# Two rotated projections: one product for the sine, the weights' high part on ScalarE, five places and a direct bank read in the local mixer

## The chip, the cores and the metric

The program runs on one core of a Trainium2 chip. The metric is the device time of one launch in microseconds (us); lower is better. PE is TensorE (matmuls), DVE is VectorE, ACT is ScalarE, POOL is GpSimd, SP is SyncE, which issues the loads here.

## What is computed

Two layers of a block with four parallel mixers. Only two of them matter here: differential attention ("a", 16 groups of width 32 for q and k together) and the windowed attention, the local mixer ("d", 6 groups of width 64). Both norm and rotate their q and k:

```python
def rmsnorm(x, g):
    y = xf * lax.rsqrt(jnp.mean(xf * xf, axis=-1, keepdims=True) + EPS)
    return (y * g).astype(x.dtype)

def _rotate(xh, ang):
    x1, x2 = jnp.split(xh, 2, axis=-1)
    return jnp.concatenate([x1 * cos - x2 * sin, x1 * sin + x2 * cos], axis=-1)

def axial_rope(x, rows, cols):      # first half of the width turned by the row, second by the column
    return concatenate([_rotate(x[..., :hd // 2], ang_r), _rotate(x[..., hd // 2:], ang_c)])

for l in range(DEPTH):              # DEPTH = 2
    px, pcx = split_cols(hx @ w_in[l]), split_cols(hc @ w_in[l])     # 1024 latent and 256 context tokens, D_MODEL 1024
    a_l, a_c = diff_attention(...); b_l, b_c = mlstm_mixer(...); c_l, c_c = gla_mixer(...); d_l, d_c = window_gqa(...)
    y = concatenate([a_l, b_l, c_l, d_l]) * silu(px[15]);  x = x + gt * (y @ w_out[l])
```

## The kernel before

The stages of a layer run one after the other, with a barrier of all engines between them. Each stage is written out by hand, engine by engine; the order in the code is the order on the engine, and counting semaphores tie the engines together. Nothing is planned by a scheduler.

`project_qk` is the stage in question. It runs four times: for "a" and for "d", in each of the two layers. The 1280 tokens are ten tiles of 128, in two halves of five (HN = 5). The product of the normed input (`hT`, channels by tokens) and a weight slab (`ring`) is made in split precision by `SplitProduct`: each operand is parted into a high part (rounded to F32R) and the low rest, and PE makes three matmuls where one would do. It goes by steps: a step is one group g (a half of the tokens and a slab) and one k of the eight 128-channel chunks. "a" has four groups (two halves with the 512 q and k columns, two halves with the 256 v columns), so 32 steps; "d" has two groups of 512 columns (384 of q and k, 128 of v), so 16 steps. I number the steps from 0. A step of 512 columns is 15 matmuls of 512 columns, a step of 256 columns is 15 of 256. For every step

- ACT makes the input's high part (`high`, line L418),
- DVE makes the weights' high part (L381), the weights' low part (L382) and then the input's low part (L435, `low`),
- PE waits for all of them and multiplies (`multiply`, L454).

The parts have three places, so that the parts of step i can be made when PE has done step i - 3.

Between the steps, work on the previous half is woven in (`half_step`): ACT squares the sums in the banks (L1427) and copies v (L1431) and q and k (L1432, to `raw`, which has five places); DVE adds the squares (L1495); ACT takes the root in two activations (L1443 and L1444, each with a table load); DVE refines it (L196 to L199, `refine`) and norms the tile (L1509). Then POOL multiplies by the gain (L1480) and makes the cosine product into `rot` (L1485), DVE makes the sine product into `turn` as four products of a quarter each (L1520) and adds both (L1528 in "a", L1534 in "d").

`rot` has two places. In "a" a place is free when DVE has added. In "d" the sum is left in `rot`, PE transposes it (`turns`, L1401, banks 6 and 7), ACT copies the result to `qkT` (L1418), and a place of `rot` is free only when PE has turned it (`turned`). PE turns tiles 0 and 1 between steps 14 and 15, and all others after step 15. In "d" the second half of the tokens has no later steps to lie beside; it is worked off after step 15.

Of the kernel before, what the change touches and what calls it, by code (L numbers as in the profile page):

```python
# [23 lines left out]
P = 128  # L24
# [360 lines left out]
class SplitProduct:  # L385
# [4 lines left out]

    def __init__(self, nc, env, own, name, groups, bufs=2):
        self.env, self.groups, self.BUFS = env, groups, bufs
        self.steps = [(g, k) for g in range(len(groups)) for k in range(KT)]
        self.first = [sum(len(q[5]) for q in groups[:g]) for g in range(len(groups) + 1)]
        self.hi, self.lo, self.weights, self.dv, self.used, self.ready, self.read = (
            env["signal"](f"{name}_{n}") for n in ("x_hi", "x_lo", "w_parts", "split", "parts_used", "sum_ready", "sum_read"))
        toks, cols = max(q[4] for q in groups), max(q[2] for q in groups)
# [12 lines left out]
    def high(self, act, i):  # L412

        g, k = self.steps[i]
        _, _, _, t0, m, _ = self.groups[g]
        if i >= self.BUFS:
            self.wait_used(act, i - self.BUFS)
        act.activation(self.x_hi[:, i % self.BUFS, 0:m], self.env["hT"][:, k, t0:t0 + m], ACT.Copy).then_inc(self.hi.sem, 1)  # L418

    def low(self, dve, i):  # L420

        g, k = self.steps[i]
        s, c0, w, t0, m, _ = self.groups[g]
        at = i % self.BUFS
        if k == 0 and (g == 0 or self.groups[g - 1][0] != s):
            dve.wait_ge(self.env["loaded"][s].sem, 16)
        if i >= self.BUFS:
            self.wait_used(dve, i - self.BUFS)
        split_weights(dve, slab(self.env, s)[:, k, c0:c0 + w], self.w_hi[:, at, 0:w], self.w_lo[:, at, 0:w], self.dv)\
            .then_inc(self.weights.sem, 1)  # L430
        if k == KT - 1 and (g + 1 == len(self.groups) or self.groups[g + 1][0] != s):
            dve.wait_ge(self.weights.sem, i + 1)
            dve.sem_inc(self.env["slab_used"].sem, 1)
        dve.wait_ge(self.hi.sem, i + 1)
        dve.tensor_tensor(self.x_lo[:, at, 0:m], self.env["hT"][:, k, t0:t0 + m], self.x_hi[:, at, 0:m].bitcast(F32),  # L435
                          ALU.subtract).then_inc(self.lo.sem, 1)
# [905 lines left out]
def project_qk(nc, env, name, s_qk, groups, width, qkT, v_of, last_slab_next, halves=None):  # L1342
# [4 lines left out]
    ps, signal = env["ps"], env["signal"]  # L1347
    n_qk = groups * width
    nch = n_qk // P
    sq_ready, reduced, ms_ready, root, normed, gained, cos_ready, rotated, dv, turned, kept = (  # L1350
        signal(f"{name}_{n}") for n in ("square", "reduced", "mean", "root", "normed", "gained", "cos", "rotated",
                                        "dve", "turned", "turned_kept"))
    s_v, v0, nv, v_dst = v_of
    HN = NT // 2
    HT = HN * P
# [4 lines left out]
    with ExitStack() as own, nc.Block() as block:  # L1360
# [8 lines left out]
        if halves:  # L1369
            rot = tile("rot", [P, 2, n_qk])  # L1370
        else:
            rot = spare[:, 3 * n_qk:5 * n_qk].rearrange("p (u c) -> p u c", u=2)
        stat = tile("stat", [P, 3, HN * groups])
        ms, rstd, tmp = (stat[:, i, :] for i in range(3))
        proj = SplitProduct(nc, env, own, f"{name}_proj", plan, 3)
        cos = C(env, f"cos_{name}").rearrange("p (t w) -> p t w", t=NT)
        sin = C(env, f"sin_{name}").rearrange("p (t w) -> p t w", t=NT)
        q4 = width // 4
# [16 lines left out]
        def _(pe):  # L1395
            def turns(t):
                pe.wait_ge(rotated.sem, t + 1)
                if t >= 2:
                    pe.wait_ge(kept.sem, t - 1)
                for c in range(nch):  # L1400
                    last = pe.transpose(ps[:, 6 + t % 2, c * P:(c + 1) * P], rot[:, t % 2, c * P:(c + 1) * P], C(env, "ident"))  # L1401
                last.then_inc(turned.sem, 1)

            for i, (g, k) in enumerate(proj.steps):
# [9 lines left out]
        def _(act):  # L1414
# [6 lines left out]
            def keep(t):  # L1421
# [40 lines left out]
            if s_v == s_qk:  # L1462
                for a in range(HN):
                    keep(HN + a)
                roots(1)
            else:
# [6 lines left out]
            act.wait_ge(proj.read.sem, proj.first[-1])  # L1473

        @block.gpsimd
        def _(pool):
            for t in range(NT):
# [12 lines left out]
        def _(dve):  # L1490
# [13 lines left out]
                rsqrt_newton(dve, dv, rstd, ms, tmp)  # L1504

            def norm(t):
                dve.wait_ge(proj.read.sem, t + 1)
                x = grouped(raw[:, t % HN, :])
                dve.tensor_tensor(x, x, of_tile(rstd, t).unsqueeze(2).broadcast_to([P, groups, width]), ALU.mult)\  # L1509
                   .then_inc(normed.sem, 1)  # L1510

            def rotate(t):
# [11 lines left out]
                dve.wait_ge(cos_ready.sem, t + 1)  # L1524
                if halves:
                    for i, half in enumerate(halves):
                        a, b = (x.rearrange("p (s i c) -> p s i c", s=2, i=2)[:, :, i, :] for x in (rot[:, t % 2, :], turn[:, :]))
                        ins = dve.tensor_tensor(half[:, t, :].rearrange("p (s c) -> p s c", s=2), a, b, ALU.add)  # L1528
                        if i == 0:
                            dv.mark(ins)  # L1530
                    dve.wait_ge(dv.sem, dv.n)
                    ins.then_inc(rotated.sem, 1)
                else:
                    dve.tensor_tensor(rot[:, t % 2, :], rot[:, t % 2, :], turn[:, :], ALU.add).then_inc(rotated.sem, 1)  # L1534

            def half_step(h, k):

# [912 lines left out]
```

## Time and profile before

| | us |
|---|---|
| median of 3 runs | 2687.75 (2673.01 to 2691.18) |
| the profiled execution, whole | 2683.7 |
| its span | 2681.9 |
| "a" in layer 0 | from 537 to 661 in the span |
| "d" in layer 0 | from 929 to 1029 in the span |

PE is busy for 2151.8 us, DVE for 1867.3, ACT for 1129.8 and POOL for 411.4 us of the span. The profile has parts on engines, on 40 slices of time, on DMA, a chain of waits, and groups of instructions by line. The trace behind it gives, for a stretch of time, who waited for whom, and every instruction with its start, its duration and, in brackets, the idle time of its engine before it and what ended that.

### The profile page before, as it was taken

The numbers are of one execution on the slowest core, as the hardware profiler recorded it, in microseconds if no ns is written. First come the engines' busy times: TensorE is split into PE (matmuls) and PEld (weight loads), VectorE is DVE, ScalarE is ACT, GpSimd is POOL, SyncE is SP. The second block draws the span as 40 slices with busy tenths as digits, with TensorE's granted clock in tenths as the row PEclk, the third lists the DMA queues.
The fourth block names the chain that finished last, engine by engine and source line by source line (L and its number), as shares of the span: only waits on it lengthen the run. The fifth ranks groups of instructions, "written<-read, shape, count | busy, mean of one in ns | idle before, by whom it ended". The sixth has DMA issues, their size and how long they took to land. (4 is left out here: it accounts for less than half of the span.)

```text
span 2681.9 us, 38569 instructions
## 1 busy us (share of the span) xinstructions
PE 2151.8 (80%) x14712; PEld 1804.3 (67%) x14712; DVE 1867.3 (70%) x3533; ACT 1129.8 (42%) x2196; POOL 411.4 (15%) x410
## 2 busy tenths in 40 slices
PE   4968798786888785899978778879767977858988
PEld 2857676666677664787857567767655866647877
DVE  2585667778878567755745766669698786667757
ACT  4433351333667534633224443432435666346321
POOL 0002204322000011022110004025031000110222
PEclk7978896898898797999988889969788989979999
DMA  8100010000000100001433000100000001000021
GB/s 322 74 16 1 17 48 2 2 1 1 1 1 1 48 32 1 29 36 39 153 138 120 16 16 2 48 16 2 1 0 1 1 1 48 16 17 27 37 104 54
DMA packets 18182, 99.80 MB, mean 37 GB/s; under 512 B 2128, under 2 KB 2256, under 8 KB 12752
## 3 DMA queue, kind: packets, MB, share of 16 engines
q1 hardware_dynamic: 12816, 87.89, 8.6%
q10 hardware_dynamic: 5184, 9.44, 0.9%
q8 instruction: 119, 1.95, 0.3%
q14 instruction: 63, 0.52, 0.1%
HBM read 87.88 MB, written 9.44 MB: 36 GB/s over the span
## 5 line engine op out<-in xcount | busy, mean ns | idle before, releaser
L1807 DVE TENSOR_REDUCE a_st<-ps 128x1 f32<-128x1280 f32 (+1 forms) x144 | 196.9, 1370 | 23.2 <-PE ps L1719 22.7
L1778 ACT ACTIVATE ring<-ps,a_st 128x1280 f32<-128x1280 f32 (+1 forms) x144 | 177.3, 1232 | 74.6 <-DVE a_st L1807 74.4
L454 PE MATMUL ps<-a_proj_wh,a_proj_xh 128*128 128x512 f32 (+1 forms) x320 | 119.2, 373 | 62.5 <-DVE a_proj_xl L435 61.6
L2090 PE MATMUL ps<-g_x_hi,g_w_hi 128*128 128x512 f32 (+1 forms) x400 | 148.4, 371 | 10.0 <-DVE g_x_lo L2151 9.5
L2091 PE MATMUL ps<-g_x_lo,g_w_hi 128*128 128x512 f32 (+1 forms) x400 | 147.7, 369 | 0.0
L2092 PE MATMUL ps<-g_x_hi,g_w_lo 128*128 128x512 f32 (+1 forms) x400 | 147.6, 369 | 0.0
L1719 PE MATMUL ps<-a_k,a_q 128*128 128x512 f32 (+1 forms) x400 | 123.8, 419 | 26.1 <-ACT ring L1778 21.6
L2151 DVE TENSOR_TENSOR g_x_lo<-hT,g_x_hi 128x512 fp32r<-128x512 f32 (+1 forms) x120 | 84.5, 709 | 85.3 <-ACT g_x_hi L2114 83.8
L2114 ACT ACTIVATE g_x_hi<-hT 128x512 fp32r<-128x512 f32 (+1 forms) x120 | 70.3, 589 | 158.3 <-PE ps L2092 151.2
L1734 PE MATMUL ps<-cst,ring 128*128 128x128 f32 x656 | 107.8, 299 | 27.0 <-ACT a_aT L1787 15.1
L418 ACT ACTIVATE b_proj_xh<-hT 128x640 fp32r<-128x640 f32 (+1 forms) x64 | 63.8, 1003 | 147.4 <-PE ps L454 145.0
L2225 PE MATMUL ps<-o_w_hi,o_y_hi 128*128 128x512 f32 x288 | 114.1, 396 | 13.5 <-DVE o_y_lo L2256 7.2
L2164 POOL TENSOR_TENSOR yT<-yT,g_gate 128x512 f32<-128x512 f32 (+1 forms) x50 | 61.3, 1232 | 382.5 <-DVE g_gate L2129 236.7
L454 PEld LDWEIGHTS ps<-a_proj_wh,a_proj_xh 128*128 128x128 f32 x320 | 68.7, 215 | 75.3 <-issue 48.9
L454 PE MATMUL ps<-a_proj_wl,a_proj_xh 128*128 128x512 f32 (+1 forms) x320 | 116.2, 363 | 0.0
L454 PE MATMUL ps<-a_proj_wh,a_proj_xl 128*128 128x512 f32 (+1 forms) x320 | 115.8, 362 | 0.0
L2226 PE MATMUL ps<-o_w_lo,o_y_hi 128*128 128x512 f32 x288 | 113.5, 394 | 0.0
L2227 PE MATMUL ps<-o_w_hi,o_y_lo 128*128 128x512 f32 x288 | 113.3, 393 | 0.0
L1734 PEld LDWEIGHTS ps<-cst,ring 128*128 128x128 f32 x656 | 81.4, 153 | 46.5 <-ACT a_aT L1787 22.9
L454 PE MATMUL ps<-b_proj_xh,b_proj_wh 128*128 128x512 f32 (+1 forms) x192 | 76.9, 401 | 44.4 <-DVE b_proj_xl L435 38.0
L418 ACT ACTIVATE a_proj_xh<-hT 128x640 fp32r<-128x640 f32 x64 | 46.6, 741 | 147.9 <-PE ps L454 145.6
L2282 ACT ACTIVATE o_y_hi<-yT 128x640 fp32r<-128x640 f32 (+1 forms) x64 | 43.5, 686 | 152.5 <-PE ps L2227 144.6
(363 smaller groups left out, 6397.9 us busy)
## 6 DMA issues: line engine op xcount, KB each, us to landing
ring<-in_w SPq DMA_DIRECT2D x22, 2048.0 KB, 7.5
yT<-in_w SPq DMA_DIRECT2D x4, 2048.0 KB, 9.8
latents<-hT ACTq DMA_DIRECT2D x32, 256.0 KB, 2.0
ring<-in_w SPq DMA_DIRECT2D x6, 1024.0 KB, 5.0
hT<-in_tok SPq DMA_DIRECT2D x10, 512.0 KB, 15.5
hT<-in_tok SPq DMA_DIRECT2D x20, 256.0 KB, 5.9
hT<-latents SPq DMA_DIRECT2D x16, 256.0 KB, 6.5
cst<-in_cst SPq DMA_DIRECT2D x1, 2688.0 KB, 14.6
```

The lines of the kernel that those rows point to most:

```text
L418: act.activation(self.x_hi[:, i % self.BUFS, 0:m], self.env["hT"][:, k, t0:t0 + m], ACT.Copy).then_inc(self.hi.sem, 1)
L454: last = pe.matmul(out, left, right, start=k == 0 and j == 0, stop=k == KT - 1 and j == 2)
L1719: last = pe.matmul(ps[:, 3 * c + b, 0:w], q4[:, 2 * h + c, t * P:(t + 1) * P], k4[:, 2 * h + c, k0:k0 + w], start=True, stop=True)
L1734: last = pe.transpose(ps[:, 6 + n % 2, (k - a) * P:(k - a + 1) * P], p(u, 0, T)[:, k * P:(k + 1) * P], C(env, "ident"))
L1778: act.activation(p(u, c, n), ps[:, 3 * c:3 * c + 3, :].rearrange("p b n -> p (b n)")[:, 0:n], ACT.Exp, bias=st[:, 0:1], accum_out=st[:, 1: ...
L1807: dve.tensor_reduce(stat[:, u % SLOTS, c, 0:1], ps[:, 3 * c:3 * c + 3, :].rearrange("p b n -> p (b n)")[:, 0:n], AX.X, ALU.max, negate=Tru ...
L2090: pe.matmul(out, w_hi[:, k, cols], x_hi[:, at, 0:b[1]], start=k == 0, stop=False)
L2091: pe.matmul(out, w_hi[:, k, cols], x_lo[:, at, 0:b[1]], start=False, stop=False)
L2092: last = pe.matmul(out, w_lo[:, k, cols], x_hi[:, at, 0:b[1]], start=False, stop=k == KT - 1)
L2225: pe.matmul(ps[:, n % 8, :], y_hi[:, at, tile], w_hi[:, at, :], start=k == 0, stop=False)
L2226: pe.matmul(ps[:, n % 8, :], y_hi[:, at, tile], w_lo[:, at, :], start=False, stop=False)
L2227: last = pe.matmul(ps[:, n % 8, :], y_lo[:, at, tile], w_hi[:, at, :], start=False, stop=k == KT - 1)
```

## The change

Five edits, all in `SplitProduct` and `project_qk`; both "a" and "d" have the first two, "d" alone the others:

1. The sine product is one instruction over the whole tile, with the axis of the two quarters read backwards, instead of four.
2. The weights' high part is made by ACT, ahead of the input's high part of the same step (`act_weights`); DVE waits for it before it makes the low part.
3. `rot` in "d" has five places instead of two. They lie in `yT[:, 6:8]` instead of the spare end of `ring`. POOL's cosine product of the first five tiles waits for no turn.
4. The second half of "d" (`late`): ACT doesn't copy q and k to `raw`; DVE's norm reads them from the banks and writes `raw`.
5. The second half of "d": DVE makes the cosine product, POOL only the gain.

```diff
     def high(self, act, i):
...
+        if self.act_weights:
+            s, c0, w = self.groups[g][0:3]
+            if k == 0 and (g == 0 or self.groups[g - 1][0] != s):
+                act.wait_ge(self.env["loaded"][s].sem, 16)
+            act.activation(self.w_hi[:, i % self.BUFS, 0:w], slab(self.env, s)[:, k, c0:c0 + w], ACT.Copy).then_inc(self.w_high.sem, 1)
         act.activation(self.x_hi[:, i % self.BUFS, 0:m], self.env["hT"][:, k, t0:t0 + m], ACT.Copy).then_inc(self.hi.sem, 1)
...
     def low(self, dve, i):
...
-        split_weights(dve, slab(self.env, s)[:, k, c0:c0 + w], self.w_hi[:, at, 0:w], self.w_lo[:, at, 0:w], self.dv)\
-            .then_inc(self.weights.sem, 1)
+        if self.act_weights:
+            dve.wait_ge(self.w_high.sem, i + 1)
+            dve.tensor_tensor(self.w_lo[:, at, 0:w], slab(self.env, s)[:, k, c0:c0 + w], self.w_hi[:, at, 0:w].bitcast(F32),
+                              ALU.subtract).then_inc(self.weights.sem, 1)
...
-            rot = spare[:, 3 * n_qk:5 * n_qk].rearrange("p (u c) -> p u c", u=2)
+            rot = env["yT"][:, 6:8, :].rearrange("p a t -> p (a t)")[:, 0:HN * n_qk].rearrange("p (u c) -> p u c", u=HN)
+        SLOTS = 2 if halves else HN
...
-        proj = SplitProduct(nc, env, own, f"{name}_proj", plan, 3)
+        proj = SplitProduct(nc, env, own, f"{name}_proj", plan, 3, act_weights=True)
...
+        def late(t):
+
+            return not halves and t >= HN
...
                 act.activation(sq[:, t % 2, :], bank[:, 0:n_qk], ACT.Square).then_inc(sq_ready.sem, 1)
+                if late(t):
+                    act.activation(v_dst(t), bank[:, v0:v0 + nv], ACT.Copy).then_inc(v_kept.sem, 1)
+                    return
...
-                if t >= 2:
-
-                    pool.wait_ge(rotated.sem if halves else turned.sem, t - 1)
-                pool.tensor_tensor(grouped(rot[:, t % 2, :]), grouped(x),
+                if late(t):
+                    continue
+                if t >= SLOTS:
+
+                    pool.wait_ge(rotated.sem if halves else turned.sem, t - SLOTS + 1)
+                pool.tensor_tensor(grouped(rot[:, t % SLOTS, :]), grouped(x),
...
-                dve.tensor_tensor(x, x, of_tile(rstd, t).unsqueeze(2).broadcast_to([P, groups, width]), ALU.mult)\
+                if late(t):
+                    dve.wait_ge(v_kept.sem, t - HN + 1)
+                    dve.wait_ge(rotated.sem, t - HN + 1)
+                dve.tensor_tensor(x, grouped(ps[:, t % BANKS, 0:n_qk]) if late(t) else x, of_tile(rstd, t).unsqueeze(2).broadcast_to([P, groups, width]), ALU.mult)\
...
-                for i in range(2):
-                    for f in range(2):
-                        ins = dve.tensor_tensor(y[:, :, f, i, :], x[:, :, f, 1 - i, :],
-                                                s[:, f, i, :].unsqueeze(1).broadcast_to([P, groups, q4]), ALU.mult)
-                        dv.mark(ins)
+                dv.mark(dve.tensor_tensor(y, x[:, :, :, ::-1, :], s.unsqueeze(1).broadcast_to([P, groups, 2, 2, q4]), ALU.mult))
+                if late(t):
+                    if t >= SLOTS:
+                        dve.wait_ge(turned.sem, t - SLOTS + 1)
+                    dv.mark(dve.tensor_tensor(grouped(rot[:, t % SLOTS, :]), grouped(raw[:, t % HN, :]),
+                                              cos[:, t, :].unsqueeze(1).broadcast_to([P, groups, width]), ALU.mult))
+                else:
+                    dve.wait_ge(cos_ready.sem, t + 1)
                 dve.wait_ge(dv.sem, dv.n)
```

What stands in a row on DVE in "d", first half, from the norms of tiles 2 to 4 to the rotation of tile 0, before (`d_proj_wh`, `wl` and `xl` are the parts of step 13, `cst` holds the sines):

```order
L1509 TENSOR_TENSOR d_raw<-d_raw,d_stat 128x384 x3
L381 CAST d_proj_wh<-ring 128x512
L382 TENSOR_TENSOR d_proj_wl<-ring,d_proj_wh 128x512
L435 TENSOR_TENSOR d_proj_xl<-hT,d_proj_xh 128x640
L1520 TENSOR_TENSOR ring<-d_raw,cst 128x6x16 x4
L1534 TENSOR_TENSOR ring<-ring 128x384
```

And in the changed kernel:

```order
L1535 TENSOR_TENSOR d_raw<-d_raw,d_stat 128x384 x3
L437 TENSOR_TENSOR d_proj_wl<-ring,d_proj_wh 128x512
L446 TENSOR_TENSOR d_proj_xl<-hT,d_proj_xh 128x640
L1544 TENSOR_TENSOR ring<-d_raw,cst 128x384
L1562 TENSOR_TENSOR yT<-yT,ring 128x384
```

The cast has left DVE, four products are one, and the sum lands in `yT`.

DVE in "d", second half, from the last line of `refine` to the first rotation, before:

```order
L198 TENSOR_SCALAR d_stat<-d_stat 128x30
L199 TENSOR_TENSOR d_stat<-d_stat 128x30
L1509 TENSOR_TENSOR d_raw<-d_raw,d_stat 128x384 x5
L1520 TENSOR_TENSOR ring<-d_raw,cst 128x6x16 x4
L1534 TENSOR_TENSOR ring<-ring 128x384
```

And in the changed kernel:

```order
L198 TENSOR_SCALAR d_stat<-d_stat 128x30
L199 TENSOR_TENSOR d_stat<-d_stat 128x30
L1535 TENSOR_TENSOR d_raw<-ps,d_stat 128x384 x5
L1544 TENSOR_TENSOR ring<-d_raw,cst 128x384
L1548 TENSOR_TENSOR yT<-d_raw,cst 128x384
L1562 TENSOR_TENSOR yT<-yT,ring 128x384
```

The norms read the banks (`ps`), and the cosine product has come to DVE between the sine product and the sum.

## Rows read from the trace of the kernel before

**Rows 1.** The page: the span, and busy time with share and instructions.
```profile
span 2681.9 us, 38569 instructions
...
PE 2151.8 (80%) x14712; PEld 1804.3 (67%) x14712; DVE 1867.3 (70%) x3533; ACT 1129.8 (42%) x2196; POOL 411.4 (15%) x410
```

**Rows 2.** Who waited for whom, 535 to 662: us in total, times, longest.
```profile
PE ps L454 <- DVE a_proj_xl L435: 30.6, 11, 6.4
```

**Rows 3.** Instructions of DVE in order of time, "a", layer 0: start, duration.
```profile
562.22 0.43 DVE L381 CAST a_proj_wh<-ring 128x512 fp32r<-128x512 f32 x1 [1.51 <-PE ps L454]
...
578.71 1.52 DVE L381 CAST a_proj_wh<-ring 128x512 fp32r<-128x512 f32 x1
580.27 1.48 DVE L382 TENSOR_TENSOR a_proj_wl<-ring,a_proj_wh 128x512 fp32r<-128x512 f32 x1
581.67 1.90 DVE L435 TENSOR_TENSOR a_proj_xl<-hT,a_proj_xh 128x640 fp32r<-128x640 f32 x1
...
589.11 0.89 DVE L1520 TENSOR_TENSOR ring<-a_raw,cst 128x128 f32<-128x128 f32 x4
...
590.93 2.88 DVE L1520 TENSOR_TENSOR ring<-a_raw,cst 128x128 f32<-128x128 f32 x4
...
627.73 0.28 DVE L381 CAST a_proj_wh<-ring 128x256 fp32r<-128x256 f32 x1
```

**Rows 4.** Instructions of POOL, the same stage.
```profile
578.27 1.69 POOL L1480 TENSOR_TENSOR a_raw<-a_raw,par 128x512 f32<-128x512 f32 x1 [67.79 <-DVE a_raw L1509]
580.03 1.17 POOL L1485 TENSOR_TENSOR a_rot<-a_raw,cst 128x512 f32<-128x512 f32 x1
581.16 1.73 POOL L1480 TENSOR_TENSOR a_raw<-a_raw,par 128x512 f32<-128x512 f32 x1
```

**Rows 5.** Instructions of ACT, the same stage.
```profile
566.30 0.60 ACT L1427 ACTIVATE ring<-ps 128x512 f32<-128x512 f32 x1
...
572.42 0.74 ACT L418 ACTIVATE a_proj_xh<-hT 128x640 fp32r<-128x640 f32 x1 [0.50 <-PE ps L454]
573.18 1.28 ACT L1443 ACT_TABLE_LOAD   x1
```

**Rows 6.** Instructions of DVE, "d", layer 0.
```profile
983.30 0.76 DVE L1520 TENSOR_TENSOR ring<-d_raw,cst 128x96 f32<-128x96 f32 x4
988.64 1.26 DVE L1534 TENSOR_TENSOR ring<-ring 128x384 f32<-128x384 f32 x1 [4.58 <-POOL ring L1485]
...
1002.78 0.56 DVE L1534 TENSOR_TENSOR ring<-ring 128x384 f32<-128x384 f32 x1 [7.44 <-POOL ring L1485]
...
1010.88 4.70 DVE L1509 TENSOR_TENSOR d_raw<-d_raw,d_stat 128x384 f32<-128x384 f32 x5
...
1026.69 0.56 DVE L1534 TENSOR_TENSOR ring<-ring 128x384 f32<-128x384 f32 x1
```

**Rows 7.** Instructions of POOL, "d", layer 0.
```profile
971.12 0.93 POOL L1485 TENSOR_TENSOR ring<-d_raw,cst 128x384 f32<-128x384 f32 x1
...
987.68 0.86 POOL L1485 TENSOR_TENSOR ring<-d_raw,cst 128x384 f32<-128x384 f32 x1 [11.03 <-PE ps L1401]
...
1001.82 0.86 POOL L1485 TENSOR_TENSOR ring<-d_raw,cst 128x384 f32<-128x384 f32 x1 [10.22 <-PE ps L1401]
```

**Rows 8.** Matmuls of PE, "d", layer 0: step 13's first, step 14's first and last, step 15's first and last.
```profile
979.00 0.47 PE L454 MATMUL ps<-d_proj_wh,d_proj_xh 128*128 128x512 f32 x1 [1.03 <-DVE d_proj_xl L435]
...
983.53 0.47 PE L454 MATMUL ps<-d_proj_wh,d_proj_xh 128*128 128x512 f32 x1 [0.84 <-DVE d_proj_xl L435]
...
986.80 0.40 PE L454 MATMUL ps<-d_proj_wh,d_proj_xl 128*128 128x512 f32 x1
...
994.81 0.77 PE L454 MATMUL ps<-d_proj_wh,d_proj_xh 128*128 128x512 f32 x1 [6.96 <-DVE d_proj_xl L435]
...
1000.92 0.42 PE L454 MATMUL ps<-d_proj_wh,d_proj_xl 128*128 128x512 f32 x1
```

**Rows 9.** Instructions of ACT, "d", layer 0: the last copy of the stage.
```profile
1028.24 0.49 ACT L1418 ACTIVATE d_qkT<-ps 128x384 f32<-128x384 f32 x1 [1.44 <-PE ps L1401]
```

More of the change, by code:

```diff
@@ L385, with __init__ @@
 class SplitProduct:
-    def __init__(self, nc, env, own, name, groups, bufs=2):
-        self.env, self.groups, self.BUFS = env, groups, bufs
+    def __init__(self, nc, env, own, name, groups, bufs=2, act_weights=False):
+        self.env, self.groups, self.BUFS, self.act_weights = env, groups, bufs, act_weights
         self.steps = [(g, k) for g in range(len(groups)) for k in range(KT)]
@@ L398, in __init__ @@
             env["signal"](f"{name}_{n}") for n in ("x_hi", "x_lo", "w_parts", "split", "parts_used", "sum_ready", "sum_read"))
+        self.w_high = env["signal"](f"{name}_w_hi")
         toks, cols = max(q[4] for q in groups), max(q[2] for q in groups)
@@ L428, in low @@
             self.wait_used(dve, i - self.BUFS)
-        split_weights(dve, slab(self.env, s)[:, k, c0:c0 + w], self.w_hi[:, at, 0:w], self.w_lo[:, at, 0:w], self.dv)\
-            .then_inc(self.weights.sem, 1)
+        if self.act_weights:
[3 more added lines that the diff above has]
+        else:
+            split_weights(dve, slab(self.env, s)[:, k, c0:c0 + w], self.w_hi[:, at, 0:w], self.w_lo[:, at, 0:w], self.dv)\
+                .then_inc(self.weights.sem, 1)
         if k == KT - 1 and (g + 1 == len(self.groups) or self.groups[g + 1][0] != s):
@@ L1349, in project_qk @@
     nch = n_qk // P
-    sq_ready, reduced, ms_ready, root, normed, gained, cos_ready, rotated, dv, turned, kept = (
+    sq_ready, reduced, ms_ready, root, normed, gained, cos_ready, rotated, dv, turned, kept, v_kept = (
         signal(f"{name}_{n}") for n in ("square", "reduced", "mean", "root", "normed", "gained", "cos", "rotated",
-                                        "dve", "turned", "turned_kept"))
+                                        "dve", "turned", "turned_kept", "v_kept"))
     s_v, v0, nv, v_dst = v_of
@@ L1400, in turns @@
                 for c in range(nch):
-                    last = pe.transpose(ps[:, 6 + t % 2, c * P:(c + 1) * P], rot[:, t % 2, c * P:(c + 1) * P], C(env, "ident"))
+                    last = pe.transpose(ps[:, 6 + t % 2, c * P:(c + 1) * P], rot[:, t % SLOTS, c * P:(c + 1) * P], C(env, "ident"))
                 last.then_inc(turned.sem, 1)
@@ L1465, in _ @@
                 roots(1)
+                act.wait_ge(v_kept.sem, HN)
             else:
@@ L1472, in _ @@
                 act.wait_ge(kept.sem, NT)
-            act.wait_ge(proj.read.sem, proj.first[-1])
+            act.wait_ge(proj.read.sem, proj.first[-1] if halves else HN)
         @block.gpsimd
@@ L1506, in norm @@
             def norm(t):
-                dve.wait_ge(proj.read.sem, t + 1)
+                if not late(t):
+                    dve.wait_ge(proj.read.sem, t + 1)
                 x = grouped(raw[:, t % HN, :])
-                dve.tensor_tensor(x, x, of_tile(rstd, t).unsqueeze(2).broadcast_to([P, groups, width]), ALU.mult)\
+                if late(t):
+                    dve.wait_ge(v_kept.sem, t - HN + 1)
+                    dve.wait_ge(rotated.sem, t - HN + 1)
+                dve.tensor_tensor(x, grouped(ps[:, t % BANKS, 0:n_qk]) if late(t) else x, of_tile(rstd, t).unsqueeze(2).broadcast_to([P, groups, width]), ALU.mult)\
                    .then_inc(normed.sem, 1)
@@ L1517, in rotate @@
                     dve.wait_ge(rotated.sem, t)
-                for i in range(2):
-                    for f in range(2):
-                        ins = dve.tensor_tensor(y[:, :, f, i, :], x[:, :, f, 1 - i, :],
-                                                s[:, f, i, :].unsqueeze(1).broadcast_to([P, groups, q4]), ALU.mult)
-                        dv.mark(ins)
+                dv.mark(dve.tensor_tensor(y, x[:, :, :, ::-1, :], s.unsqueeze(1).broadcast_to([P, groups, 2, 2, q4]), ALU.mult))
[4 more added lines that the diff above has]
+                                              cos[:, t, :].unsqueeze(1).broadcast_to([P, groups, width]), ALU.mult))
+                else:
+                    dve.wait_ge(cos_ready.sem, t + 1)
                 dve.wait_ge(dv.sem, dv.n)
-                dve.wait_ge(cos_ready.sem, t + 1)
                 if halves:
                     for i, half in enumerate(halves):
-                        a, b = (x.rearrange("p (s i c) -> p s i c", s=2, i=2)[:, :, i, :] for x in (rot[:, t % 2, :], turn[:, :]))
+                        a, b = (x.rearrange("p (s i c) -> p s i c", s=2, i=2)[:, :, i, :] for x in (rot[:, t % SLOTS, :], turn[:, :]))
                         ins = dve.tensor_tensor(half[:, t, :].rearrange("p (s c) -> p s c", s=2), a, b, ALU.add)
@@ L1533, in rotate @@
                 else:
-                    dve.tensor_tensor(rot[:, t % 2, :], rot[:, t % 2, :], turn[:, :], ALU.add).then_inc(rotated.sem, 1)
+                    dve.tensor_tensor(rot[:, t % SLOTS, :], rot[:, t % SLOTS, :], turn[:, :], ALU.add).then_inc(rotated.sem, 1)
             def half_step(h, k):
```

## The prediction

> **What bounds the kernel now.** The stages are parted by barriers, so each is read by itself, and a gain in one goes through to the end. The page says only that PE is busy for 80% and DVE for 70% of the span [rows 1]. The waits of "a" in layer 0 say more: PE stood 30.6 us for DVE's last part of a step [rows 2]. At first that isn't so. In the order of time DVE makes a step's parts and then idles 1.51 us for PE [rows 3]: PE bounds the first half of "a". Once the norms and rotations are woven in, DVE has no such gap, and PE waits. In "d" the reader should look at three waits: DVE for POOL's cosine product, 4.58 and 7.44 us [rows 6]; POOL, ahead of those products, 11.03 and 10.22 us for a turn on PE [rows 7]; PE, ahead of step 15, 6.96 us for DVE [rows 8]. That is one ring: two places of `rot`, freed only by turns that PE does late. After 1010.88 there is no projection left, and DVE works alone to 1028.73, the end of the last copy [rows 6, 9].
>
> **A price that changes the sum.** Beside POOL a cast took 1.52 us, alone 0.43 [rows 3]. The ends show why. POOL's gain ended at 578.27 + 1.69 = 579.96, the cast 0.27 later; the cosine product ended at 581.20, DVE's next operation at 581.75; the second gain at 582.89, the one after at 583.57 [rows 3, 4]. The two take turns; each waits for the other's operation and then needs its own short time. So a cast that is removed there gives back about 0.3 to 0.4, not 1.5: POOL's operation then stands ahead of the next DVE operation instead. Only if POOL runs dry earlier is the rest won.
>
> **The cast, moved to ACT.** DVE loses 0.43 (512 columns) or 0.28 (256 columns) in each step [rows 3]. It counts only where DVE is last. In "a" these are steps 12 to 15 (4 x 0.4 = 1.6) and about 8 of the 16 steps with 256 columns (8 x 0.3 = 2.4); the others wait for PE or ACT anyway. ACT gains about 0.60, by the row of 512 columns [rows 5], some 0.4 at 256. Mostly its idle time covers that. It shows where ACT is last: before the roots ACT goes from the high part (572.42) straight into the table load (573.18) [rows 5], so in "a" the roots come 0.7 later in the first half and 0.5 in the second, and one more step behind the copies of v 0.4 later: together 1.6. The later start also puts one more POOL operation between the norms: 0.9, the size of one POOL operation less what it overlaps. At the stage's start DVE now waits for ACT: 0.15, below what I carry.
>
> **The sine product.** Four took 0.89 us in "a" and 0.76 in "d", beside POOL up to 2.88 [rows 3, 6]. No row shows one of 512 with a reversed axis. A subtraction of 512 ends 0.55 after POOL lets go (581.20 to 581.75), and I take 0.55 to 0.6 for the product: the four do as many elements, in the same short runs. So 0.3 per tile is won in "a", 0.3 in "d". For the tiles beside POOL the ends are 0 (turns are taken as before) and 2.88 - 0.6 = 2.3; I take 0.3, since four products let POOL in once or twice, and its work remains. "a": 10 x 0.3 = 3.0.
>
> **Sum for "a".** 1.6 + 2.4 + 3.0 - 1.6 - 0.9 = 4.5 us per layer, with bounds of 0 (ACT's delay takes it all) and 11.5 (every removed instruction at the duration in its row).
>
> **"d", first half.** POOL now has five more operations in a row (cosine products of tiles 2, 3, 4, gains of 3, 4), each some 0.85 to 0.93 [rows 7], and DVE takes turns with them instead of running alone. By walking the two queues, with 0.55 and 0.68 for DVE's parts and 0.45 for a norm, DVE gives step 13's last part at 980.2, so PE starts it at 980.3 instead of 979.00, and step 14 at 986.05 instead of 983.53 [rows 8]. A loss first. Then the ring is gone: the rotations of tiles 2 and 3 take 1.2 us each with no wait, DVE has step 15's parts at 989.9, and PE, done with step 14 after 3.5 us and with two turns after 0.75, starts step 15 at 990.3 instead of 994.81. Step 14 took 3.7 us and step 15, after 6.96 idle, 6.5 (994.81 to the end of the last matmul at 1001.34): the matmuls ran at the lower of the two clock levels, 0.77 for the first against 0.47 [rows 8]. Without the wait I give it 3.5, so it ends at 993.8 instead of 1001.34.
>
> **"d", between the halves.** DVE no longer stands 7.44 us in the rotation of tile 4 [rows 6]. The squares follow the tiles through step 15. Behind its end come the last square, sum and mean (1.3), the roots with their table loads (2 x 1.28 [rows 5], 3.1 with the activations) and `refine` (0.9): the norms start at 999.2 instead of 1010.88. Gain: 11.7.
>
> **"d", second half.** It took 1028.73 - 1010.88 = 17.85. Norms: five in 4.70 beside POOL [rows 6]; read from the banks I keep that price and add 0.2. POOL's gains end about 2.3 later, and the first rotation, now with a cosine product on DVE, ends 3.3 after the norms. Four rotations follow at 0.5 + 0.5 + 0.56 + 0.1 = 1.64, that is 6.55; turn and copy add 1.5. Together 16.2: DVE has 0.5 more per tile, but waits no more for POOL and turns. Gain: 1.6. For the bank read the ends are 2.3 (five at 0.45) and 7 (five at 1.4).
>
> Here the trace has no row of DVE reading a bank beside POOL. The Trainium skill ("SBUF — State Buffer", "Who interferes with whom") says that a DVE instruction with two SBUF inputs takes turns with a GpSimd instruction that reads SBUF, and one with at most one SBUF input doesn't. The norm of the late tiles has one. By that rule the five norms would take some 2.6 us and leave POOL alone, and the rest would follow 1.6 us earlier in each layer.
>
> **Sum.** "d": 11.7 + 1.6 = 13.3 per layer. Both stages in both layers, which look alike in the trace: 2 x (4.5 + 13.3) = 35.6. The profiled execution took 2683.7, so 2648.1; the median of 2687.75 stands 4 higher, which gives 2652.
>
> **Rivals.**
> - *Bank reads don't take turns.* As above, 3.2 less: 2649. The same case for all practical ends.
> - *Durations at face value.* If POOL runs dry early enough that what I call turns vanishes with the instructions, "a" gives 11.5 and "d" 16: 55 together, 2633. For it: the pair of queues is often idle in "a". Against: the ends of the rows match turn for turn.
> - *POOL's unbroken train cools PE.* Steps 13 and 14 are each preceded by a wait of 1.5 to 2.5 us, where 1.03 and 0.84 stood. If the granted clock then falls as it did ahead of step 15, steps 13 to 15 take up to 3 us more each, and "d" gives 6.5: 22 together, 2666.
> - *ACT's new work is in the way.* "a" gives nothing and "d" loses 2: 2 x 11.3 = 23, 2665. For it: DVE's first operation of a step now hangs on ACT, behind squares and table loads. Against: ACT's idle time elsewhere in these stages.
> - *Slower: the product with the reversed axis.* If one such instruction costs well over the four, all 40 pay on DVE, which bounds these stretches. The point is 35.6 / 40 + 0.6 + 0.3 = 1.8 us each. At 2.88, the highest row of four, each costs 2.3 more than my 0.6, or 92 for 40: 2652 + 92 = 2744. Against: the four alone run at 0.89 with the same runs of 8 and 16 elements.
>
> **How the numbers follow.** Main case 0.35 (2652), bank reads without turns 0.20 (2649), face value 0.18 (2633), cooled PE 0.12 (2666), ACT in the way 0.11 (2665), slower 0.04. A measurement of this kernel can tell about 1%, 27 us, from no change: the line is at 2661. The main cases lie 9 to 12 us under it, and 0.05 of their chance goes over. So faster 0.55 - 0.05 + 0.18 + a share of 0.05 from the two at 2665 = 0.73; same 0.23; slower 0.04. The range takes in face value and the two cases with half the gain: 2629 to 2668.
>
> **What would show it.** Right: in "d" no DVE wait for POOL's cosine product in the first half; POOL with ten operations in a row; step 15 of 3.5 us within a microsecond of step 14's turns; the last copy about 13 us earlier after the stage's start. In "a" PE's wait for DVE shrinks from 30.6 to some 26. Wrong: a product over 1 us alone; DVE's low part waiting for ACT in the bound stretches; late norms over 1 us each; steps 13 and 14 with first matmuls of 0.77.

## The result and the profile after

The changed kernel takes 2644.98 us (median of 4 runs, 2643.67 to 2652.88); the kernel before, run between them, 2684.22 (4 runs, 2673.01 to 2691.18). The ratio is 0.9863, 95% interval 0.9835 to 0.9890: faster by 1.1 to 1.65%. The profiled execution took 2645.6 us, against 2683.7. One run of all those below was disturbed (edit 2 alone, 4105.53 us, its four others 2656.72 to 2675.35 with a median of 2662.10): it is in that kernel's median and not in its ratio. The page, in the lines of [rows 1]:

```profile
span 2643.8 us, 38509 instructions
...
PE 2147.0 (81%) x14712; PEld 1801.3 (68%) x14712; DVE 1820.2 (69%) x3327; ACT 1168.7 (44%) x2282; POOL 411.8 (16%) x400
```

DVE has lost 47 us and ACT won 39. The span lost 38.1, which says nothing yet about where. So I read the stages one by one, from a stage's first matmul to the first instruction of the next (in "d", to the next stage's first work on PE):

| us | before | changed | difference |
|---|---|---|---|
| "a", layer 0 and 1 | 122.08, 125.01 | 119.34, 118.53 | -9.2 |
| "d", layer 0 and 1 | 98.84, 97.66 | 83.46, 83.92 | -29.1 |
| all the rest of the span | 2238.3 | 2238.6 | +0.3 |

The +0.3 is a sum of differences both ways: the stage ahead of "a" in layer 0 alone is 5.4 us shorter in the changed kernel, and others are longer (see the end). So the edits are read from their own stages, not from the whole.

**Stage "d", first half, layer 0.** The matmuls of steps 13 and 15, as [rows 8], now stand so in the order of time:

```profile
969.25 0.47 PE L465 MATMUL ps<-d_proj_wh,d_proj_xh 128*128 128x512 f32 x1 [2.44 <-DVE d_proj_xl L446]
...
978.88 0.48 PE L465 MATMUL ps<-d_proj_wh,d_proj_xh 128*128 128x512 f32 x1
```

No wait stands ahead of step 15 where 6.96 us stood. The windows over step 15 before, and then over steps 13, 14 and 15 of the changed kernel, show the clock as well (columns: length, busy time of PE, PEld, DVE, ACT, POOL, granted clock, DMA share, GB/s):

```profile
994.81:1001.34 6.53, 6.53 (x17) 5.08 (x18) 0.53 (x4) 2.08 (x6) 0.00 (x0) 0.53 0.79 309
```
```profile
969.25:974.50 5.25, 5.25 (x15) 3.86 (x15) 4.94 (x6) 0.00 (x0) 2.92 (x3) 0.67 0.00 0
974.80:978.30 3.50, 3.49 (x15) 2.87 (x16) 3.04 (x6) 0.00 (x0) 0.00 (x0) 1.00 0.00 0
978.88:982.60 3.72, 3.72 (x20) 3.03 (x19) 2.65 (x6) 3.46 (x10) 0.00 (x0) 1.00 0.90 348
```

The clock granted in step 15 was 0.53, nearly all at the lower level (1.2 GHz), and is 1.00 now. Step 13 pays: after its wait of 2.44 it stands at 0.67 and takes 5.25 instead of 3.7. In layer 1 the slow step is the next one, step 14, here its first matmul and its window:

```profile
2310.72 0.47 PE L465 MATMUL ps<-d_proj_wh,d_proj_xh 128*128 128x512 f32 x1 [1.89 <-DVE d_proj_xl L446]
```
```profile
2310.72:2316.00 5.28, 5.28 (x17) 4.16 (x18) 4.45 (x8) 0.00 (x0) 0.00 (x0) 0.68 0.30 87
```

**Stage "d", second half, layer 0.** DVE, in order of time, as [rows 6]:

```profile
987.36 2.41 DVE L1535 TENSOR_TENSOR d_raw<-ps,d_stat 128x384 f32<-128x384 f32 x5
989.69 0.79 DVE L1544 TENSOR_TENSOR ring<-d_raw,cst 128x384 f32<-128x384 f32 x1
990.40 1.34 DVE L1548 TENSOR_TENSOR yT<-d_raw,cst 128x384 f32<-128x384 f32 x1
...
999.37 0.55 DVE L1548 TENSOR_TENSOR yT<-d_raw,cst 128x384 f32<-128x384 f32 x1
999.95 0.56 DVE L1562 TENSOR_TENSOR yT<-yT,ring 128x384 f32<-128x384 f32 x1
```

The last copy, as [rows 9], on ACT:

```profile
1001.51 0.49 ACT L1434 ACTIVATE d_qkT<-ps 128x384 f32<-128x384 f32 x1 [1.24 <-PE ps L1417]
```

Five norms from the banks take 2.41 us beside POOL where they took 4.70. Counted from the stage's first matmul (931.02 before, 919.67 now), the norms start 12.2 earlier (79.86 to 67.69), the last copy ends 15.4 earlier (97.71 to 82.33). In layer 1 it is less: 10.5 (78.67 to 68.15) and 13.7 (96.53 to 82.79).

**Stage "a", layer 0.** The waits of the stage, as [rows 2], PE first, then DVE (us in total, times, longest):

```profile
PE ps L465 <- DVE a_proj_xl L446: 26.1, 10, 5.8
```
```profile
DVE a_proj_wl L437 <- ACT a_proj_wh L423: 21.6, 13, 4.2
```

PE's wait for DVE went from 30.6 to 26.1. The same stage grouped by line, operation and shape (count, busy us, mean ns, idle time ahead) shows where the rest of DVE's relief went. Before:

```profile
L1520 DVE TENSOR_TENSOR ring<-a_raw,cst 128x128 f32<-128x128 f32 x40 | 14.8, 430 | 0.5
L1509 DVE TENSOR_TENSOR a_raw<-a_raw,a_stat 128x512 f32<-128x512 f32 x10 | 10.4, 1083 | 0.1
...
L381 DVE CAST a_proj_wh<-ring 128x512 fp32r<-128x512 f32 x16 | 7.9, 493 | 11.1 <-PE ps L454 11.1
...
L1528 DVE TENSOR_TENSOR yT<-a_rot,ring 128x256 f32<-128x256 f32 x10 | 4.2, 425 | 0.3
```

Changed:

```profile
L1535 DVE TENSOR_TENSOR a_raw<-a_raw,a_stat 128x512 f32<-128x512 f32 x10 | 12.5, 1300 | 0.1
L437 DVE TENSOR_TENSOR a_proj_wl<-ring,a_proj_wh 128x512 fp32r<-128x512 f32 x16 | 12.1, 756 | 16.9 <-ACT a_proj_wh L423 16.9
...
L1544 DVE TENSOR_TENSOR ring<-a_raw,cst 128x512 f32<-128x512 f32 x10 | 7.9, 794 | 0.5
L1556 DVE TENSOR_TENSOR yT<-a_rot,ring 128x256 f32<-128x256 f32 x10 | 7.1, 714 | 1.0
```

The product lost 6.9 us of busy time, but the norms show 2.1 more and the first halves of the sums 2.9 more (the second halves, written to `a_qk`, went from 4.2 to 6.3), though nothing in them was edited. Together that is as much as the product lost. Their rows contain turns with POOL, and the turns have moved into them. And DVE, which before idled for PE, now idles 21.6 us for ACT. Where ACT is itself held by PE, which has to free the parts, that is the old idle time under another name (12.2 us, in ten waits for PE, before). The version with ACT in some steps, below, tells how much of it is more.

### The profile page after: what moved, and what is told of

It is laid out like the page before. It is cut to its first block and busy times, and to the rows that moved or that the text cites. A ratio compares the mean times of both kernels' runs of the same rounds, so it can differ in the third digit from the quotient of the medians.

```text
span 2643.8 us, 38509 instructions
## 1 busy us (share of the span) xinstructions
PE 2147.0 (81%) x14712; PEld 1801.3 (68%) x14712; DVE 1820.2 (69%) x3327; ACT 1168.7 (44%) x2282; POOL 411.8 (16%) x400
## 5 line engine op out<-in xcount | busy, mean ns | idle before, releaser
L424 ACT ACTIVATE b_proj_xh<-hT 128x640 fp32r<-128x640 f32 (+1 forms) x64 | 63.8, 1003 | 146.4 <-PE ps L465 144.1
L465 PEld LDWEIGHTS ps<-a_proj_wh,a_proj_xh 128*128 128x128 f32 x320 | 68.5, 214 | 65.6 <-issue 55.7
L1217 ACT ACTIVATE yT<-ps 128x1024 f32<-128x1024 f32 x40 | 41.0, 1024 | 147.9 <-PE ps L1235 147.9
## 6 DMA issues: line engine op xcount, KB each, us to landing
hT<-in_tok SPq DMA_DIRECT2D x10, 512.0 KB, 15.4
```

The source lines that it names most:

```text
L465: last = pe.matmul(out, left, right, start=k == 0 and j == 0, stop=k == KT - 1 and j == 2)
```

## The experiments

All times are medians of rounds in which the kernel before ran between (its medians there were 2679.28, 2680.23 and 2680.17, and the ratios are taken against those). The column "edited stages" is the sum of the four stages of "a" and "d" in the profiled execution, minus that of before (443.6). It doesn't contain what other stages do by themselves.

| kernel | us | ratio, 95% | edited stages |
|---|---|---|---|
| changed | 2644.98 | 0.9863 [0.9835, 0.9890] | -38.3 |
| changed, repeated | 2647.08 | 0.9880 [0.9865, 0.9895] | -39.3 |
| before, repeated | 2690.34, one run | | +0.2 |
| edit 1 alone | 2657.61 | 0.9916 [0.9892, 0.9939] | -12.7 |
| edit 2 alone | 2666.60 | 0.9936 [0.9896, 0.9977] | -6.2 |
| edit 3 alone | 2664.55 | 0.9932 [0.9908, 0.9956] | -16.0 |
| edits 1, 2, 3 | 2652.56 | 0.9896 [0.9872, 0.9920] | -33.8 |
| edits 1 to 4 | 2648.17 | 0.9871 [0.9828, 0.9913] | -40.2 |
| edits 1, 2, 3, 5 | 2646.17 | 0.9872 [0.9855, 0.9888] | -33.7 |
| changed, ACT in some steps | 2635.04 | 0.9835 [0.9806, 0.9865] | -42.4 |
| the same, repeated | 2637.76 | 0.9850 [0.9825, 0.9876] | -42.1 |

### Edit 1 alone: the product

```diff
-        proj = SplitProduct(nc, env, own, f"{name}_proj", plan, 3, act_weights=True)
+        proj = SplitProduct(nc, env, own, f"{name}_proj", plan, 3)
...
-            return not halves and t >= HN
+            return False
...
-        SLOTS = 2 if halves else HN
+        SLOTS = 2
```

(`rot` has its two places in the spare end of `ring` again.)

> The kernel before with the first edit alone: one sine product instead of four, in both stages; casts on DVE, two places, no late path. Theory of turns (POOL and DVE wait for each other's operation, and only DVE's own short time is won): a product alone in 0.55 to 0.7 us instead of 0.76 to 0.89, 0.3 us per tile wherever DVE is last; 'a' 2 to 3 us less per layer, 'd' 1.5 to 2 (its tail alone, five tiles), together some 9 us less. Face value (what the rows of four products beside POOL lasted is won in full, 2.88 to under 1): 'a' 6 to 8 less per layer, together some 20. Slow reversed axis: a product alone above 1.2 us, and the kernel slower than before.

The edited stages gave 12.7 us, between the 9 of the theory of turns and the 20 of face value. In "a" the last low part came 117.45 and 116.52 us after the stage's first matmul. The three kernels that leave "a" alone (before, its repeat, edit 3 alone) have 118.9 to 121.1 there, mean 120.0. So the product is worth 3.0 per layer, the figure that I had taken, known to about a microsecond: stages of one kind lie up to 1.1 off their mean. In "d" it gave 3.5 and 2.2, more than the 1.5 to 2 that I had expected from its tail alone. The tail, from the first norm to the last copy, gave 1.3 in each layer (17.85 to 16.52). Most of the rest came before it, where step 15 took 5.16 us in both layers instead of 6.53 and 6.14, after a wait of 6.64 instead of 6.96: the granted clock over it was 0.69, not 0.53 and 0.57. Its rows, on DVE in order of time, show no price for the reversed axis:

```profile
579.90 0.69 DVE L1543 TENSOR_TENSOR ring<-a_raw,cst 128x512 f32<-128x512 f32 x1
```

0.69 us alone, against 0.89 for the four. The median moved by more, 22 us. The trace puts part of the rest into stages that the edit doesn't touch: the one ahead of "a" in layer 0 was 5.2 us shorter, the one ahead of "d" in layer 1 6.3 (see the end).

### Edit 2 alone: ACT makes the weights' high part

```diff
-                dv.mark(dve.tensor_tensor(y, x[:, :, :, ::-1, :], s.unsqueeze(1).broadcast_to([P, groups, 2, 2, q4]), ALU.mult))
+                for i in range(2):
+                    for f in range(2):
+                        ins = dve.tensor_tensor(y[:, :, f, i, :], x[:, :, f, 1 - i, :],
+                                                s[:, f, i, :].unsqueeze(1).broadcast_to([P, groups, q4]), ALU.mult)
+                        dv.mark(ins)
```

(With `return False` and `SLOTS = 2` as above, `act_weights=True` kept.)

> The kernel before with the second edit alone: ACT makes the weights' high part in 'a' and 'd'. Theory of turns: DVE wins 0.3 to 0.4 a step where it is last, ACT's roots come 0.5 to 1.4 later in each half; 'a' 0 to 2 us less per layer, 'd' 0.5 to 1 more; the whole within 4 us of before. Face value (a cast beside POOL is worth its 1.2 to 1.5 us): 'a' 5 less per layer, 'd' 1 less, 12 in all.

The edited stages gave 6.2 us: more than the 4 of the theory of turns, half of the 12 of face value. Most of it lies in "a", where the last low part came at 117.89 and 117.19: 2.5 per layer. The step that lies between the norms, with POOL at work, on DVE:

```profile
578.43 1.29 DVE L1534 TENSOR_TENSOR a_raw<-a_raw,a_stat 128x512 f32<-128x512 f32 x2
579.64 1.79 DVE L437 TENSOR_TENSOR a_proj_wl<-ring,a_proj_wh 128x512 fp32r<-128x512 f32 x1
581.35 1.72 DVE L446 TENSOR_TENSOR a_proj_xl<-hT,a_proj_xh 128x640 fp32r<-128x640 f32 x1
583.00 5.00 DVE L1534 TENSOR_TENSOR a_raw<-a_raw,a_stat 128x512 f32<-128x512 f32 x3
```

From the start of the first norm to the end of the fifth there are 9.57 us (578.43 to 588.00). The kernel before took 9.90, with a cast of 1.52 among them [rows 3]. Removing it returned 0.33; in "d" 7.92 became 7.59. The instruction that follows the cast has grown from 1.48 to 1.79, and the norms behind it have grown too. These stretches bear out the turns; which steps gave the rest of the 6.2 us is not shown.

### Edit 3 alone: five places

```diff
-        SLOTS = 2
+        SLOTS = 2 if halves else HN
```

(Against the kernel before, with the places in `yT[:, 6:8]`.)

> The kernel before with the third edit alone: five places for the rotation's result in 'd'; four products, casts on DVE, second half through raw and POOL. Theory of the ring: step 15 of 'd' starts 4 to 5 us earlier after the stage's start and lasts 3.7 us instead of 6.5, the norms of the second half start 11 to 12 us earlier, and 'd' is 11 to 13 us shorter per layer, 'a' unchanged; 24 us in all. If instead the second half (bank reads and the cosine product on DVE) carried the gain, 'd' would be at most 5 us shorter here, 10 in all.

"d" became 8.8 and 7.5 us shorter, with none of the other edits: less than the 11 to 13 expected, more than the at most 5 of the rival. The cosine products of the first five tiles wait for no turn, so step 15's parts are there soon after PE is done with step 14. PE, in order of time:

```profile
991.32 0.82 PE L1417 MATMUL ps<-cst,yT 128*128 128x128 f32 x6
992.66 0.47 PE L465 MATMUL ps<-d_proj_wh,d_proj_xh 128*128 128x512 f32 x1 [0.52 <-DVE d_proj_xl L446]
```

Step 15's wait fell from 6.96 to 0.52, and its first matmul stands at the upper level of the clock. The wait is still DVE's: with the casts and four products its low part of step 15 is done 60.6 after the stage's first matmul, in the changed kernel at 59.0. So step 15 starts 3.0 earlier than before (60.8 against 63.8, layer 0), not the 4 to 5 expected, and the tail behind the first norm is no shorter than before (18.3). Step 13 shows PE at the lower clock here too: after a wait of 3.04 us step 13 took 6.44 at a granted clock of 0.54, where it had taken 3.69. It cost only 0.3, since step 14's low part was done at 55.7 and the step began at 56.0. This is the largest of the edits: the ring of two places was the limit there.

### Edits 1, 2 and 3 together

```diff
         def late(t):
-            return not halves and t >= HN
+            return False
```

> The changed kernel without its fourth and fifth edits: the second half of 'd' goes through raw and POOL's cosine product as before, all else as changed. Theory of the ring: most of the gain stays; 'd' is 2 to 3 us longer per layer than in the changed kernel (norms at 4.7 us for five instead of 2.4, and POOL's ten operations in turns with DVE), so 4 to 6 us slower than the changed kernel, some 34 us faster than before. If the late path were what matters, it would lose 10 us or more.

-33.8 us in the edited stages; the three alone add up to -34.9. They hardly overlap. What edits 4 and 5 add together is the rest to the changed kernel: 4.5 and 5.5 us by its two profiles, 2.3 to 3.5 in each "d".

### Edits 4 and 5 apart

Edits 1 to 4, POOL makes the late cosine product:

```diff
-                if late(t):
-                    continue
...
-                if late(t):
-                    if t >= SLOTS:
-                        dve.wait_ge(turned.sem, t - SLOTS + 1)
-                    dv.mark(dve.tensor_tensor(grouped(rot[:, t % SLOTS, :]), grouped(raw[:, t % HN, :]),
-                                              cos[:, t, :].unsqueeze(1).broadcast_to([P, groups, width]), ALU.mult))
-                else:
-                    dve.wait_ge(cos_ready.sem, t + 1)
+                dve.wait_ge(cos_ready.sem, t + 1)
```

> The changed kernel without its fifth edit: late norms read the banks, but POOL makes the late cosine products (ten POOL operations in the second half of 'd', two DVE operations per rotation instead of three). Theory of turns: the norms stay at 2.4 us for five; then POOL's 8.7 us and DVE's products and sums go in turns, so the tail from the first norm to the last copy is within 1 us of the changed kernel's 14.6. If moving the cosine product to DVE is what pays, the tail is 3 us or more longer.

Edits 1, 2, 3 and 5, the norms read `raw`, which ACT fills as before:

```diff
-                if late(t):
-                    act.activation(v_dst(t), bank[:, v0:v0 + nv], ACT.Copy).then_inc(v_kept.sem, 1)
-                    return
...
-                dve.tensor_tensor(x, grouped(ps[:, t % BANKS, 0:n_qk]) if late(t) else x, of_tile(rstd, t).unsqueeze(2).broadcast_to([P, groups, width]), ALU.mult)\
+                dve.tensor_tensor(x, x, of_tile(rstd, t).unsqueeze(2).broadcast_to([P, groups, width]), ALU.mult)\
```

> The changed kernel without its fourth edit: ACT copies the late tiles to raw and the norms read raw; DVE makes the late cosine products. Theory that a norm with one operand in a bank takes no turns with POOL: here five norms last 4.5 to 5 us instead of 2.4, and 'd' is 1.5 to 2.5 us longer per layer, 3 to 5 in all. Rival (the norms were faster only because POOL started later): they last about 2.5 us here too, and 'd' is the same.

The bank read pays and the moved cosine product doesn't. Without edit 5, "d" is as long as in the changed kernel (83.0 and 84.0 against 83.5 and 83.9). Without edit 4 it is as long as without both (85.9 and 86.1 against 86.4 and 86.2). Of the 2.2 to 3.4 us that edit 4 gives in a "d", 1.7 to 1.8 lie in the tail (16.3 to 16.5 without it, 14.6 to 14.8 with it). The rest lies ahead of the norms, which start 0.5 to 1.6 earlier; that ACT has no copies of q and k to make there would explain it, but no run parts the two. DVE's rows of the five norms and what follows, first of the kernel without edit 4, then without edit 5:

```profile
994.02 4.82 DVE L1527 TENSOR_TENSOR d_raw<-d_raw,d_stat 128x384 f32<-128x384 f32 x5
998.76 1.34 DVE L1536 TENSOR_TENSOR ring<-d_raw,cst 128x384 f32<-128x384 f32 x1
```
```profile
986.27 2.41 DVE L1533 TENSOR_TENSOR d_raw<-ps,d_stat 128x384 f32<-128x384 f32 x5
988.60 0.66 DVE L1542 TENSOR_TENSOR ring<-d_raw,cst 128x384 f32<-128x384 f32 x1
989.37 1.16 DVE L1554 TENSOR_TENSOR yT<-yT,ring 128x384 f32<-128x384 f32 x1
990.63 1.03 DVE L1542 TENSOR_TENSOR ring<-d_raw,cst 128x384 f32<-128x384 f32 x1
```

Five norms with both inputs in SBUF take 4.82 beside POOL's gains, five with one input in a bank 2.41 beside the same gains. This is what the Trainium skill ("SBUF — State Buffer", "Who interferes with whom") says: outside the 2-port modes a DVE instruction with at most one SBUF input doesn't contend with GpSimd, and one with two contends with a GpSimd instruction that reads SBUF. In the last two rows a product and a sum that take 0.56 alone take 1.03 and 1.16 between POOL's operations; that is the price of leaving the cosine product on POOL, and it equals that of five more products on DVE: from the first norm to the end of the last sum it is 13.28 us here (986.27 to 999.55) and 13.15 in the changed kernel (987.36 to 1000.51).

### Where ACT's work is in the way

DVE's 21.6 us of waiting for ACT in "a" left a question: is ACT's new operation late anywhere it matters? In this version ACT makes the weights' high part in some steps only: not in a stage's first group, and not in steps where squares, copies or roots are due; there DVE casts again.

```diff
+    def by_act(self, i):
+
+        g, k = self.steps[i]
+        return self.act_weights and g >= 1 and k not in ((1, 2) if g == 3 else (1, 2, 3))
...
-        if self.act_weights:
+        if self.by_act(i):
...
-            dve.wait_ge(self.w_high.sem, i + 1)
+            dve.wait_ge(self.w_high.sem, sum(self.by_act(n) for n in range(i + 1)))
```

> The changed kernel, but ACT makes the weights' high part only in the steps where it has time and DVE is last; DVE makes it in the whole first group and in the steps just ahead of the roots and of the copies of v (steps 1 to 3 of the second and third group, 1 and 2 of the fourth). Theory that ACT's new work delays the roots: DVE's refinement starts 1 us or so earlier in each half, 'a' is 1 to 2 us shorter per layer than in the changed kernel, 'd' 0.5 to 1; 3 to 6 us in all. Rival (ACT's work is covered): within 1 us of the changed kernel, or slower, since DVE has casts again.

The last low part in "a" comes at 112.84 and 113.93, against a mean of 115.6 in the kernels with edits 1 and 2 throughout. DVE's waits for ACT's high parts in "a", layer 0, have mostly gone:

```profile
DVE a_proj_wl L442 <- ACT a_proj_wh L428: 4.2, 2, 2.3
```

Its waits for PE are back, 9.5 us in seven. So of the 21.6 us some 8 were new waiting, and the rest was the old idle time. The first `refine` starts 36.3 and 36.7 after the stage's first matmul, where with edit 2 in all steps it starts at 38.0 on average.

The edited stages are 3 to 4 us shorter than in the changed kernel. The median, 2635.04, is 10 us lower, so most of that lay elsewhere. The same kernel was therefore run again, beside the changed one, and the kernel before was profiled once more:

> The variant in which ACT makes the weights' high part in some steps only, once more. Theory that ACT delayed the roots: 'a' again takes 113 to 114 to DVE's last part, where the changed kernel took 115.4 to 116.3, and 'd' 82 to 83 to its last copy; 3 to 5 us under the changed kernel, where the stages without edits agree, so 2640 to 2645. If the 12 us by which its median lay under the changed kernel's were its own, they come again in the stages 'a' and 'd'; if they come in other stages or not at all, they weren't.

> The changed kernel once more, on the chip and beside the runs of the three variants, to compare them with: about 39 us faster than before; stages without the edits may differ by some us from one execution to the next.

> The kernel before, profiled once more. Seven profiles showed that stages without an edit come in two lengths some 5 to 10 us apart (from the first matmul of the gated linear attention's projection to that of 'a': 213 or 218 us in layer 0, 206.5 or 216.3 in layer 1), and the changed kernel's two profiles agreed in nearly all of them. If the length belongs to the kernel, this profile repeats 218.2 and 216.3; if to the execution, at least one of the two differs. 'a' (from its first matmul to DVE's last part) should take 119 to 121, 'd' (to the last copy) 96.5 to 98.

Repeated, it took 2637.76, and its edited stages -42.1: again some 3 us better than the changed kernel's -38.3 and -39.3. The last low part in "a" came at 113.54 and 114.31. Over its four stages that part comes 2.0 earlier on average than in the ten of the kernels with edits 1 and 2 throughout, yet the stages are only 1.0 shorter (117.6 against 118.7), as PE ends 3.4 instead of 2.2 us behind the last low part in three of the four. Single stages overlap (one of the ten had 114.24). By its median this is the fastest version measured, both times. The intervals of its ratios (0.9806 to 0.9865 and 0.9825 to 0.9876) overlap with those of the changed kernel, so the 3 us in the edited stages are shown by two profiles of each kernel, and the 9 to 10 us in the median are not shown to belong to the edit.

## Why the prediction was right, point by point

2652 was forecast, 2629 to 2668 as the range; 2645 was measured. 2.7 of the 7 us lie in the edited stages (38.3 instead of 35.6). Half of the 7 is the base: I added 4 us for the median of before as it then stood, 2687.75, and with the later runs it is 2684.22.

- **The casts' price: turns, not durations.** Shown. I took 0.3 to 0.4 for a cast beside POOL whose row says 1.52; the stretch around it became 0.33 to 0.36 shorter in each kernel with edit 2. The rival at face value would have had 55 us. It fell, and with it the busy column as a guide: DVE's 47 us less and the span's 38 are near each other by chance, since 29.1 of the 38 came in "d", where waits went.
- **"a": 4.5 per layer.** The last low part came 4.4 earlier (mean of ten stages with both edits, 115.6, against six with neither, 120.0); the stages became 4.6 shorter. The terms: products 3.0, measured 3.0. Casts less ACT's delay less one POOL operation, 1.6 + 2.4 - 1.6 - 0.9 = 1.5; measured alone 2.5, on top of the product 1.4. ACT's delay of the first roots, 0.7 taken: `refine` starts 0.8 later in the mean of twelve stages with edit 2 than in eight without, 38.0 against 37.2, with single stages up to 0.8 off their mean. PE's wait for DVE, some 26 forecast, is 26.1.
- **"d", first half: a loss first.** The signs named for it came: DVE has no wait for POOL's cosine product there, and POOL's ten operations stand in a row (959.36 to 972.25). The walk of the two queues gave step 13 a start of 49.3 after the stage's first matmul (980.3 less 931.02), step 14 of 55.0 and step 15 of 59.3. Measured: 49.6, 55.1, 59.2 in layer 0, and 48.4, 54.0, 59.7 in layer 1. The rival in which the train of POOL's operations cools PE was half right. In layer 0 step 13 took 5.25 at a granted clock of 0.67. It ended 0.3 before step 14's parts were ready, so this cost nothing, and steps 14 and 15 ran at 1.00. In layer 1 step 13 ran at 1.00 and step 14, after a wait of 1.89, took 5.28 at 0.68. Step 15 followed it without a gap, though its low part was there at 57.87: an estimated 1.6 us lost (5.28 less the 3.7 at the upper level). The sign named for this rival, a first matmul of 0.77, is missing in the changed kernel's first profile and stands at step 13 of layer 0 in its repeat.
- **"d", to the norms.** Forecast 11.7 earlier, measured 12.2 in layer 0 and 10.5 in layer 1. That the two layers are alike holds to within 2 us: the last copy came 15.4 and 13.7 earlier, with 13.3 forecast.
- **"d", second half: the mis-sized term.** I took 16.2 us with the norms at 4.70 plus 0.2. It took 14.6 (67.69 to 82.33), in both layers. The norms took 2.41, 2.5 less; the four rotations behind the first took 7.50 instead of 6.55, since the second still met POOL's gains. So the tail was 1.6 shorter than my sum, as I had written for the rule on bank reads, and the total by that rule, 2649, was the nearest of all the cases. I had also written that the trace has no row of DVE reading a bank beside POOL. It has, in another stage. DVE, then POOL, of the kernel before:

```profile
1303.39 0.69 DVE L2244 TENSOR_TENSOR o_prod<-ps,gate_rows 128x512 f32<-128x512 f32 x1 [0.89 <-POOL hT L2269]
```
```profile
1303.23 1.30 POOL L2269 TENSOR_TENSOR hT<-hT,o_prod 128x512 f32<-128x512 f32 x1
```

  The DVE instruction lies wholly inside POOL's, and takes the 0.69 that it takes alone. This row gave the price of the norms before any run. The row that I took was one of an instruction with two SBUF inputs.
- **ACT in the way.** As a case of its own it fell ("a" gave its 4.5). In small it is there: the version with ACT in some steps got back 2.0 us per "a" stage up to the last low part, and 1.0 of the stage's length.
- **The product with the reversed axis.** 0.69 in "a", 0.55 in "d" where POOL is idle. The slower case fell.

## What to carry to other kernels

An instruction's duration beside POOL is a turn plus its own short time: price its removal by the ends of the rows around it, and move an input into a bank rather than the work to another engine if the turns are what costs. One SBUF input isn't enough of a test: the norm with one took no turns (2.41 for five), the cast with one did (1.52 beside POOL, 0.43 alone [rows 3]). Look for a row of the same kind anywhere in the trace before you price by the nearest one in the stage. A ring of buffers that is freed by the last engine in a chain (here PE's turns, behind its own next step) can cost more than any instruction in it (edit 3 was the largest here): look for the engine that waits for a release, and count the places. When work goes to an idle engine, its steps that stand behind that engine's bursts may be better left where they were (here 3 us of the edited stages).

## What was not expected of the hardware

Stages that no edit touches come in two lengths, several us apart, though their instructions are the same. The stage ahead of "a" (windows of two kernels in layer 0, before and changed, then of two in layer 1, changed and ACT in some steps; the seventh number is the granted clock):

```profile
322.00:540.00 218.00, 179.84 (x1885) 152.84 (x1885) 161.78 (x310) 74.14 (x129) 51.22 (x43) 0.84 0.05 18
```
```profile
319.00:531.00 212.00, 171.29 (x1884) 145.91 (x1883) 160.23 (x307) 73.96 (x130) 52.41 (x43) 0.88 0.05 18
...
1662.00:1879.00 217.00, 179.91 (x1881) 153.22 (x1882) 161.06 (x306) 72.94 (x125) 51.91 (x43) 0.84 0.05 19
```
```profile
1671.00:1877.00 206.00, 167.20 (x1880) 142.51 (x1880) 159.25 (x304) 72.28 (x123) 53.07 (x43) 0.91 0.05 19
```

As many matmuls take 8.6 and 12.7 us less of PE's time, and the stage follows. In layer 0 it lasted 218.2 to 218.3 in before (twice), in edit 2 alone, in edits 1 to 3 and in the first profile of ACT in some steps, and 212.7 to 213.1 in the seven others. In layer 1 the lengths are 216.3 to 216.5 (eight profiles) and 206.4 to 209.0 (four). Before and the changed kernel each repeated theirs in a second profile; the version with ACT in some steps did not, in either layer (218.33 and 212.90, 206.52 and 216.39). So a length belongs neither to the edits nor wholly to the kernel. What decides it stays open. In the result it cancels: the stages outside "a" and "d" together differ by 0.3 us between before and changed. For edit 1 alone it doesn't, and that is why the edits are compared here by their own stages.
